# Reordering the step of the first expert stage in a two-layer attention, recurrence and mixture-of-experts kernel, with smaller routing tables and a second weight buffer

## What is computed

```python
def swiglu(t, wg, wu, wd):
    return (jax.nn.silu(t @ wg) * (t @ wu)) @ wd

    scores = jax.nn.sigmoid(t.astype(f32) @ router_w.astype(f32))
    ...
    _, idx = lax.top_k(jnp.where(expert_mask, sel, -jnp.inf), TOP_K)
    w = jnp.take_along_axis(scores, idx, axis=1)
    w = w / jnp.sum(w, axis=-1, keepdims=True) * ROUTED_SCALE
    ...
    def expert_block(args):
        tok_b, w_b, e = args
        yb = swiglu(t_pad[tok_b], w_gate[e], w_up[e], w_down[e])
        return yb.astype(f32) * w_b[:, None]
```

## Time and profile before

| | |
|---|---|
| runs, median (lowest to highest) | 2322.23 us (2318.98 to 2324.4) |
| the profiled execution | 2321.31 us |
| its span, first to last instruction | 2319.5 us |
| PE busy / DVE busy / ACT busy | 1913.9 / 1148.0 / 792.0 us |
| first expert stage, its passes | 469.3 to about 1188 us |
| second expert stage | 1713 to 2264 us |

### The profile page before, as it was taken

How to read it: one execution, slowest core, us unless ns; L and a number is a source line. 1 busy time by engine, 2 the same in 40 slices (tenths; PEclk the granted TensorE clock), 3 DMA queues, 4 the chain that set the end, 5 groups by cost and what they waited for, 6 DMA issues and landing times. The chain is left out here.

```text
span 2319.5 us, 33553 instructions
## 1 busy us (share of the span) xinstructions
PE 1913.9 (83%) x9971; PEld 1296.5 (56%) x9972; DVE 1148.0 (49%) x2243; ACT 792.0 (34%) x1283; POOL 317.4 (14%) x333
## 2 busy tenths in 40 slices
PE   2899997889999999999975887637778787788883
PEld 0778844467777777777742881103445555555551
DVE  2325622577777777777748565893131121111124
ACT  1214511155555556555521456870101111111110
POOL 0220010021211111121110102221001111111110
PEclk9999997989999999999987997768879999999997
DMA  6850054069999899999956416304439999999994
GB/s 240 282 202 2 1 224 180 32 230 333 340 332 339 324 339 348 346 334 343 336 179 249 136 47 202 110 19 131 183 145 415 407 402 404 404 404 392 409 381 173
DMA packets 139045, 597.07 MB, mean 257 GB/s; under 512 B 32632, under 2 KB 51128, under 8 KB 79728
## 3 DMA queue, kind: packets, MB, share of 16 engines
q1 hardware_dynamic: 103264, 509.97, 58.5%
q0 software_dynamic: 35584, 84.31, 9.8%
q10 hardware_dynamic: 144, 2.10, 0.2%
HBM read 596.17 MB, written 56.20 MB: 281 GB/s over the span
## 5 line engine op out<-in xcount | busy, mean ns | idle before, releaser
L1459 DVE TENSOR_TENSOR m_w_lo<-m_wgu,m_w_hi 128x1024 fp32r<-128x1024 f32 x264 | 314.0, 1221 | 157.3 <-ACT m_w_hi L1383 146.3
L1383 ACT ACTIVATE m_w_hi<-m_wgu 128x1024 fp32r<-128x1024 f32 x264 | 269.7, 1053 | 192.9 <-DMA m_wgu<-in_moe_w_up 135.2
L1630 PE MATMUL ps<-m_wgu,m_xT 128*64 128x256 f32 x2112 | 263.0, 405 | 77.4 <-DMA m_wgu<-in_moe_w_up 57.0
L1630 PEld LDWEIGHTS ps<-m_wgu,m_xT 128*64 128x64 f32 x2112 | 187.3, 146 | 164.0 <-issue 117.2
L1325 PE MATMUL ps<-m_wd,m_hidT 128*128 128x512 f32 x528 | 237.6, 593 | 0.3 <-ACT m_hidT L1407 0.3
L1340 PE MATMUL ps<-m_w_hi,m_x_hi 128*128 128x512 f32 x528 | 212.7, 403 | 7.1 <-DVE m_x_lo L1451 7.0
L1340 PE MATMUL ps<-m_w_lo,m_x_hi 128*128 128x512 f32 x528 | 208.1, 394 | 0.0
L1340 PE MATMUL ps<-m_w_hi,m_x_lo 128*128 128x512 f32 x528 | 207.2, 392 | 0.0
L1725 DVE SCALAR_TENSOR_TENSOR m_hid<-m_act_g,m_meta,ps 128x256 f32<-128x256 f32 x33 | 15.8, 480 | 337.7 <-ACT m_act_g L1679 337.7
L1325 PEld LDWEIGHTS ps<-m_wd,m_hidT 128*128 128x128 f32 x528 | 95.3, 190 | 95.1 <-issue 95.1
L1266 POOL DMA_INDIRECT y_rows<-h,m_sidx x66 | 67.5, 1023 | 552.8 <-DVE h L1467 552.8
(11 more groups left out here) (317 smaller groups left out, 3420.5 us busy)
## 6 DMA issues: line engine op xcount, KB each, us to landing
m_wgu<-in_moe_w_gate SPq DMA_DIRECT2D x132, 1024.0 KB
m_wgu<-in_moe_w_up SPq DMA_DIRECT2D x132, 1024.0 KB
m_wd<-in_moe_w_down SPq DMA_DIRECT2D x132, 1024.0 KB, 9.7
c_rows<-y_rows SPq DMA_DIRECT2D x12, 2048.0 KB, 16.1
mods<-in_ada_w POOLq DMA_DIRECT2D x11, 1024.0 KB, 7.3
mods<-in_ada_w SPq DMA_DIRECT2D x11, 1024.0 KB, 4.8
mods<-in_lru_w_in SPq DMA_DIRECT2D x7, 1280.0 KB, 6.9
ada_w<-in_ada_w SPq DMA_DIRECT2D x8, 1024.0 KB, 17.8
```

Source lines behind the costliest of these rows:

```text
L1383: act.activation(w_hi[:, :, k, :], wgu[:, q, :, k, :], ACT.Copy).then_inc(hi_s, 1)
L1459: dve.tensor_tensor(w_lo[:, :, k, :], wgu[:, q, :, k, :], w_hi[:, :, k, :].bitcast(F32), ALU.subtract).then_inc(lo_s, 1)
L1630: last = pe.matmul(g.ps[half[s], GU, a * FE:(a + 1) * FE], xT[:, k, half[s]], wgu[:, s, a, k, :], start=(k == 0), stop=(k == KD - 1))
```

## The change

Four things are changed together.

1. `entry` becomes bfloat16, each of its three numbers as a sum of three pieces (nine columns). The one-hot matrix becomes bfloat16 and is made by one DVE instruction per block in place of four. `indices` sums the pieces by a reduction, and then makes the gather's index from the sum. The router phase writes the pieces.
2. First expert stage, PE: the token transposes go behind chunk 1 and the slot products behind chunk 2. The down product is cut in two halves, j = 0 ahead of the small transposes and j = 1 behind them. `y_done` comes with the second half. `hidT` gets two buffers.
3. First stage, ACT and DVE: both take the tokens of block b+1 behind chunk 1; DVE takes the indices of b+3 behind chunk 2, ahead of the hidden rows; ACT takes the copy of the hidden rows ahead of the output half. POOL issues a gather ahead of the scatter it used to follow.
4. Second expert stage: gate and up weights get two buffers and the second pair's are prefetched too; down weights keep one.

```diff
-        self.entry = sb(n + "entry", [P, tiles, EXPERTS, 3])
+        self.entry = sb(n + "entry", [P, tiles, EXPERTS, 3 * PIECES], BF16)
...
-        self.wgu = sb(tag + "wgu", [P, 2, 2, KD, FE])
+        self.wgu = sb(tag + "wgu", [P, 2, 2, 2, KD, FE])
...
+                for m in range(PIECES):
+                    piece = routes.entry[:, :, :, GAIN * PIECES + m]
+                    chain.link(dve.tensor_copy(piece, weight[:]))
+                    if m + 1 < PIECES:
+                        chain.link(dve.tensor_tensor(weight[:], weight[:], piece, ALU.subtract))
...
+        TURN_AT, SLOTS_AT = 1, 2
...
-        hidT = sb("hidT", [P, KF, S])
+        hidT = sb("hidT", [P, 2, KF, S])
...
                 with pool.Fori(1, final + 1) as i:
+                    gather(i + 1, 1)
                     scatter(i - 1, 1)
-                    gather(i + 1, 1)
+                    gather(i + 2, 0)
                     scatter(i, 0)
-                    gather(i + 2, 0)
...
                         last.then_inc(chunk_used, 1)
-                    turn_tokens(i + q, 1 - q)
+                        if c == TURN_AT:
+                            turn_tokens(i + q, 1 - q)
+                        if c == SLOTS_AT:
+                            slots(i + 1 + q, 1 - q)
                     if not first:
-                        down(i - 1 + q, 1 - q, first=(isinstance(i, int) and i == 0 and q == 1))
+                        down(i - 1 + q, 1 - q, 0, first=(isinstance(i, int) and i == 0 and q == 1))
                     pe.wait_ge(hid_s, b + 1)
...
                     last.then_inc(hid_turned, 1)
-                    slots(i + 1 + q, 1 - q)
+                    if not first:
+                        down(i - 1 + q, 1 - q, 1)
...
                     if split:
-                        split_low(i + q, 1 - q, range(CHUNKS - 1))
+                        split_low(i + q, 1 - q, range(TURN_AT + 1))
+                    tokens(i + q, 1 - q)
+                    if split:
+                        split_low(i + q, 1 - q, range(TURN_AT + 1, CHUNKS - 1))
+                    indices(i + 1 + q, 1 - q)
...
                     if split:
                         split_low(i + q, 1 - q, range(CHUNKS - 1, CHUNKS))
-                    tokens(i + q, 1 - q)
                     if not first:
                         y_half(i - 1 + q, 1 - q, wait=not first_y)
                     pick(i + 2, q)
-                    indices(i + 1 + q, 1 - q)
...
+                with sp.Fori(0, turns) as m:
+                    gate_up(2 * m + 1, 0)
+                    down(2 * m + 1)
+                    gate_up(2 * m + 2, 1)
+                    down(2 * m + 2)
```

More of the change, by code:

```diff
@@ L930, in prefetch @@
     def prefetch(self, sp):
-        for s in range(2):
-            self.gate(sp, s, s)
-        for s in range(2):
-            self.up(sp, s, s)
-        for s in range(2):
-            self.down(sp, s, s)
+        for q in range(2):
+            for s in range(2):
+                self.gate(sp, 2 * q + s, q, s)
+            for s in range(2):
+                self.up(sp, 2 * q + s, q, s)
+            if q == 0:
+                for s in range(2):
+                    self.down(sp, s, s)
 def route_phase(g, layer, tiles, routes, weights):
@@ L1364, in _ @@
                     step(i, 1)
-                down(final, 1)
+                for j in range(KF):
+                    down(final, 1, j)
             @block.scalar
@@ L1587, in _ @@
                 pool.wait_ge(zeroed, 1)
[L1588 removed]
+                turns = rounds(pool)
                 gather(0)
```

185 lines of the change are left out of this document (107 added, 78 removed).

## The result

| | before | after |
| --- | --- | --- |
| median of the runs, us | 2320.76 (2310.95 to 2324.4, 8 runs) | 2329.63 (2324.73 to 2333.2, 8 runs) |
| ratio to before | 1 | 1.0043, interval 1.0031 to 1.0055 |
| span of the profiled execution, us | 2319.5 | 2326.5 |
| mean step of the first expert stage, us | 10.94 | 11.15 |
| first stage, first pass of the weights, us from the start | 469.35 | 468.91 |

The change makes the kernel slower by 0.43%, some 9 us. 2337 us was forecast, in a range of 2298 to 2354.

What follows compares the result with a forecast made beforehand. PE was taken to bound the first expert stage, DMA close behind, and DMA the second. 2321.3 us + 23 (longer first-stage steps) - 3 (head) - 5 (second stage) gave 2336, as a median 2337 us, range 2298 to 2354.

Steps and rivals of the forecast that it cites:

- Which chain sets the step: First expert stage: late weight cast at t, then hidden rows, small transposes, half down product; step ends at t + 8.56 us.
- How t answers: First stage, t being the cast's start in its step: issue to cast 12.3 us, step 11.30, +23 us over 64 steps.
- Gather ahead of scatter: First stage, POOL: earlier gather may fill dry DMA engines, between no gain and 0.3 us a step; 0.06 taken.
- Minimum of a step: First stage: even with weights in time, the second low part behind chunk 1 puts the step at 10.49 us.
- One-hot, slot products: First stage: one-hot in one DVE instruction gains nothing; four bfloat16 slot products take 0.20 us instead of 0.81.
- Head of the first stage: Before the first pass: shorter slot products and one-hots save 3.5 us, router phase costs 0.5; net -3.0 us.
- Second stage: Second expert stage: slot products and one-hots -1.5, earlier gate/up load less tail wait -3.2, shorter tables -0.3; sum -5.0 us.
- The sum: Whole kernel: 2321.3 + 23 - 3 - 5 = 2336 us, median 0.9 above the profiled run, so 2337 us.
- rival 4: Second stage keeps its whole 10.4 us from earlier gate/up loads beside the slower first stage: 2330 us; chance 0.04.
- The first: Rival, first stage: DMA absorbs the later issue, step falls to 10.49 us, total 2285 us; chance 0.12.
- The third: Rival, first stage: time from issue to use stays whole, step 11.56 us, total 2354 us; chance 0.12.
- The second: Rival, first stage: issue-to-use time shrinks by 1.0 to 1.5 us, step stays 10.94, total 2314 us; chance 0.20.

Runs made afterwards that it cites:

- e5: Changed kernel with both halves of the down product ahead of the small transposes: 2310.6 us, ratio 0.9956.
- e1: Changed kernel with SP issuing the next gate and up weights ahead of the down weights: 2294.0 us, ratio 0.9873.
- e2: Changed kernel with the first stage's old step order on PE, ACT, DVE and POOL, keeping bfloat16 tables: 2310.1 us, ratio 0.9955.
- e6: Changed kernel with DVE's reduction and index back at the step's end, behind the hidden rows: 2327.7 us, ratio 1.0038.
- e12: Changed kernel with POOL issuing scatter ahead of gather again: 2355.9 us, ratio 1.0148.
- e9: Changed kernel with old step order, gate and up weights issued first, and the bfloat16 table stored piece by piece: 2265.5 us against 2270.3 without the table edit.
- e8: Changed kernel with old step order, gate and up issued first, and one second-stage gate/up buffer, prefetching one pair: 2272.8 us against 2270.3 with two buffers.
- e10: e9 with a second buffer for the second stage's down weights too: 2246.1 us, ratio 0.9678.

## Why the prediction was right, and where it was not

**Which chain sets the step: right.** Hidden rows behind the cast, PE idle ahead of the small transposes, the half product at the end, later issues. The chain from the cast to the next step's real start is 8.72 us (8.39 as printed) against 8.56 forecast, and the issue is at 1.94 (2.27 printed) against 1.86. e5 shows that the half product costs 19 us, and e1 that SP's order costs 36, of which the change itself brought only a part. The mean cast is at 2.4 (2.74 printed) against 2.8, and the DMA share is 0.89 as forecast. PE waited for the hidden rows 37.1 us over 43 steps and not 60 over all, since some 20 steps were at their minimum.

**How t answers: right in kind, too long in size.** This term was put at 12.3 us and measured 11.63. With it alone the forecast's own sum gives a step of (1.86 + 11.63 + 8.56) / 2 = 11.03; the later issue and the longer chain bring it to 11.15. So the step was not the 11.30 forecast, and the 62 steps gave +13 us and not the +23 of the sum: an error of the term was in part made up by two smaller ones. This is the largest error, and the same term misled e2 and e5 the other way (12.8 there). It is no constant, and no rule found here gives it: it was 12.8 at steps of 10.8 to 10.9, 11.6 at 11.2, 12.0 at 11.2 with the gather late (e6) and 12.5 at the longest steps, of 11.6 (e12). The forecast's reduction from 12.7 by mean share alone gave the direction, but a third of the size.

**Gather ahead of scatter, taken at 0.06 us a step: wrong.** It is worth 26 us in the new order (e12), because it lets the gathered rows arrive for the earlier transposes and the weights' time is 0.9 us shorter with it (why is not shown). I had compared the issue's gain of 4 us with the use's gain of 2.7, and not asked what would be late if the issue stayed.

**Minimum of a step: 10.49 forecast, 10.61 measured**, and reached in about 20 steps.

**One-hot, slot products: right.** 0.26 us for four products against 0.20 taken; the register load in mid-pass cost nothing that shows.

**Head of the first stage, -3.0: wrong.** The first pass came only 0.4 us earlier, which one trace can't tell from nothing: the other kernels with the same router phase and head have it at 467.4 to 471.2 us. The head itself gained about 2.5 us, but the router phase grew by about 2.1, for which I had put back 0.5: I priced the casts by the gain's write of 0.51 us, whose values lie 12 bytes apart, and a bfloat16 write 18 bytes apart takes 0.73 (e9). Not foreseen at all: the first two steps became 3.0 us shorter (23.9 to 20.9).

**Second stage, -5.0: too much.** From the second router phase on, the kernel gained 1.6 us: 8.6 late ahead of it, 7.0 late at the end. The stage itself gave 2.3 of the forecast 3.5, no more than such stages differ from trace to trace (e8), and the head lost its 1.5 to the second router phase. That the second buffer is not worth its whole 10.4 us was right, by e8.

**The sum.** +13 in place of +23, -3.4 in place of -3 up to the third step, about -2.8 in place of -5 behind the last: +7 by the spans against +15.7. The traces bear these parts only roughly: in the second layer's recurrence, which the change does not touch, the distance between the two goes from 9.5 us to 5.5 and back to 8.6. The result lies in the forecast's own 2328 to 2348, but at its lower end: a little over half of the 16 us that were forecast. That it lies there at all is in part luck: the head gave 0.4 of its 3.0 us, and the first two steps, which the forecast had no term for, gave the other 3.0. The median also lies on rival 4's 2330, whose mechanism did not occur.

**The rivals.** The first (DMA absorbs the later issue, 2285) fell: the cast came at 2.74 and PE waited 37 us for the hidden rows. No kernel with late casts had a mean of less than 11.6 us from issue to cast. The Trainium skill (DMA: Bandwidth & Descriptors, Anatomy of one DMA) has a rule for one DMA of the GpSimd path, by which the three weights would take an estimated 9.2 us. The traces, in which SP issues them among other transfers, do not agree: two of the three took 11.6 us and more. The third (2354) fell with the measured 11.63. The second (2314) had its condition met: the time shrank by 1.2 us from the 12.79 of before, within its 1.0 to 1.5. But its sum took 11.45 and the forecast's issue and chain, and from the measured three the step is 11.15 and not 10.94; its time did not come. The fourth (whole 10.4 us kept) fell by e8. But the first had a true core that I did not use: with the issue moved ahead instead of behind, the step is at its minimum (e1).

## What to carry over

When a chain runs once round a loop (issue, arrival, cast, end of the step, next issue), look first at what the issue waits for: here two lines of SP's order, with a reason to wait for the low parts only, were worth 36 to 40 us where the step was short of weights and 3 where PE was full, and the whole rearrangement nothing. Put work that can cover a wait behind the awaited instruction, but nothing that the end of the step needs. And before an operation is moved earlier, list what it consumes and when that was issued.

## What the runs showed of the hardware beyond the forecast

- The time from the issue to the use of 2 MB of weights (1 MB each, gate and up) in this traffic was 11.6 to 12.8 us on average in the kernels whose casts were late. Neither the length of the step nor the place of the gather orders these values (12.80 in e5, 12.52 in e12).
- A full DMA moved 403 GB/s in the second stage, at nearly the same share 418 when the down weights had a second buffer (e10).
- A DVE write of 128 by 256 bfloat16 values took 0.29 us side by side and 0.73 us at a stride of 18 bytes.
- In the second stage PE's granted clock was 0.98 in the window before and 0.90 after, where PE idles in one piece ahead of the down product, and that product took 5.31 us in place of 3.65. From 2234.60 to 2240.00, the stretch of that product, it was 0.69 of the 2.4 GHz level, so part of it ran at 1.2 GHz. It is 0.95 to 0.96 again with one buffer for everything (e8) or two for everything (e10). Inside the stage, where DMA is busy all the time, no run parts what those 1.7 us cost; in the tail after the change PE's own work is all that is left from 2250.76 on, and there they add to the time: 18.6 us in place of e9's 16.8.
